# Six more modulation blocks reduced across the partitions by GpSimd instead of TensorE, with one accumulator for all of them

## What is computed

```python
mod = jax.nn.silu(c) @ w_ada[l] + b_ada[l]                 # 2048 x 12288
sh_a, sc_a, gt_a, sh_f, sc_f, gt_f = jnp.split(mod, 6, axis=-1)
h = rmsnorm(x, g_pre_attn[l]) * (1.0 + sc_a) + sh_a        # needed at once
...
x = x + gt_a * rmsnorm(mix @ w_out[l], g_post_attn[l])     # needed at the output projection
h = rmsnorm(x, g_pre_ffn[l]) * (1.0 + sc_f) + sh_f         # needed before the feed-forward part
f = (jax.nn.silu(h @ w_gate[l]) * (h @ w_up[l])) @ w_down[l]
x = x + gt_f * rmsnorm(f, g_post_ffn[l])
```

## Time and profile before

| | us |
|---|---|
| time, median of 3 runs (lowest, highest) | 2506.98 (2505.96, 2508.56) |
| time of the profiled execution | 2507.84 |
| its span | 2506.1 |
| PE busy | 2382.0 (95%) |
| DVE busy | 1670.5 (67%) |
| ACT busy | 1135.2 (45%) |
| POOL busy | 95.2 (4%) |

### The profile page before, as it was taken

How to read it: one execution, slowest core, us unless ns; L and a number is a source line. 1 busy time by engine, 2 the same in 40 slices (tenths; PEclk the granted TensorE clock), 3 DMA queues, 4 the chain that set the end, 5 groups by cost and what they waited for, 6 DMA issues and landing times.

```text
span 2506.1 us, 27346 instructions
## 1 busy us (share of the span) xinstructions
PE 2382.0 (95%) x10764; PEld 1966.3 (78%) x10764; DVE 1670.5 (67%) x1789; ACT 1135.2 (45%) x1473; POOL 95.2 (4%) x62
## 2 busy tenths in 40 slices
PE   2799999979999999899969999999999999999997
PEld 2577787868888888788858888888888888888886
DVE  6988898968888888755554555656555555555564
ACT  3345566554444444444453433443445544444453
POOL 1000000001111111300000000000000001000000
PEclk7899999989999999999989999999999999999999
DMA  8988788959999999755535655555566557665553
GB/s 297 366 298 310 269 289 335 350 181 334 325 335 327 327 329 325 267 188 198 191 125 167 208 180 181 183 189 176 199 205 205 198 193 256 205 196 190 186 190 111
DMA packets 255317, 600.52 MB, mean 240 GB/s; under 512 B 12313, under 2 KB 12633, under 8 KB 248673
## 3 DMA queue, kind: packets, MB, share of 16 engines
q1 hardware_dynamic: 252224, 589.43, 67.5%
q0 software_dynamic: 2976, 9.49, 1.2%
HBM read 596.74 MB, written 2.13 MB: 239 GB/s over the span
## 4 chain that ended last, share of the span: by engine, by line
PE 89%; DVE 6%; ACT 2%; DMA 2%; issue 1%; SPq 0%; DVEq 0%; ACTq 0%
PE PS L1181 19%; PE PS L1182 18%; PE PS L1187 18%; PE PS L1153 10%; PE PS L1156 10%; PE PS L1162 10%; DVE BIAS L1594 3%; DMA RAW<-in_w_in 1%; PE PS L1252 1%; DMA RAW<-in_w_ada 1%; DVE LO L1576 1%; ACT HI L687 1%; PE PS L1509 1%; PE PS L1278 0%; PE PS L1224 0%
## 5 line engine op out<-in xcount | busy, mean ns | idle before, releaser
L1576 DVE TENSOR_TENSOR LO<-RAW,HI 128x1024 fp32r<-128x1024 f32 x808 | 1013.8, 1260 | 726.2 <-ACT HI L687 724.9
L687 ACT ACTIVATE HI<-RAW 128x1024 fp32r<-128x1024 f32 x808 | 854.4, 1059 | 1213.3 <-PE PS L1187 746.8
L1181 PE MATMUL PS<-HI,XH 128*128 128x512 f32 x2176 | 871.1, 400 | 29.6 <-ACT HI L687 29.6
L1182 PE MATMUL PS<-HI,XL 128*128 128x512 f32 x2176 | 856.5, 394 | 0.0
L1187 PE MATMUL PS<-LO,XH 128*128 128x512 f32 x2176 | 585.9, 391 | 0.0
L1181 PEld LDWEIGHTS PS<-HI,XH 128*128 128x128 f32 x2176 | 413.3, 190 | 121.2 <-DVE XL L1720 20.9
L1187 PEld LDWEIGHTS PS<-LO,XH 128*128 128x128 f32 x2176 | 411.5, 189 | 87.6 <-DVE LO L1576 0.3
L1182 PEld LDWEIGHTS PS<-HI,XL 128*128 128x128 f32 x2176 | 414.0, 190 | 83.8 <-issue 1.0
L1594 DVE SCALAR_TENSOR_TENSOR BIAS<-RAW,CACT,BIAS 128x1024 f32<-128x1024 f32 x270 | 346.3, 1283 | 8.6 <-DMA RAW<-in_w_ada 1.4
L1153 PE MATMUL PS<-HI,XH 128*128 128x512 f32 x1056 | 328.5, 392 | 4.0 <-ACT HI L687 4.0
L1156 PE MATMUL PS<-HI,XL 128*128 128x512 f32 x1056 | 326.6, 391 | 0.0
(11 more groups left out here) (285 smaller groups left out, 998.6 us busy)
## 6 DMA issues: line engine op xcount, KB each, us to landing
RAW<-in_w_in SPq DMA_DIRECT2D x208, 1024.0 KB, 5.0
RAW<-in_w_ada SPq DMA_DIRECT2D x112, 1024.0 KB, 6.0
RAW<-in_w_gate SPq DMA_DIRECT2D x88, 512.0 KB, 4.5
RAW<-in_w_up SPq DMA_DIRECT2D x88, 512.0 KB, 5.5
RAW<-in_w_down SPq DMA_DIRECT2D x44, 1024.0 KB, 4.8
RAW<-in_w_ada SPq DMA_DIRECT2D x64, 512.0 KB, 6.0
RAW<-in_w_out SPq DMA_DIRECT2D x32, 1024.0 KB, 5.2
RAW<-in_w_proj_b SPq DMA_DIRECT2D x16, 1024.0 KB, 5.1
```

Source lines behind the costliest of these rows:

```text
L687: act.activation(HI[:, (it["half"] + hf) % HLS, :], RAW[:, it["slot"], hf * 1024:(hf + 1) * 1024], ACT.Copy).then_inc(s.hi_ready, 1)
L1181: pe.matmul(PS[:, bank + u, :], XH[:, 2 * n + kk, rows], hi, start=start and kk == 0, stop=False)
L1182: pe.matmul(PS[:, bank + u, :], XL[:, 2 * n + kk, rows], hi, start=False, stop=False)
L1576: dve.tensor_tensor(LO[:, slot, :], RAW[:, it["slot"], hf * 1024:(hf + 1) * 1024], HI[:, slot, :].bitcast(F32), ALU.subtract).then_inc(s.l ...
```

## The change

`ADA_BY_PE` goes from 10 to 4: TensorE sums groups 0 to 3 alone, GpSimd sums groups 4 to 17. So from group 4 on one accumulator `ACC` serves all groups, and the other is `SUM`. Groups 4, 5, 6 and 9 (sh_f and sc_f) go through memory: row 0 of `SUM` to `mod_dram`, back into `MODT` as 32 rows of 128, one transpose on TensorE into PSUM behind the last half of the first stage, and one add to `SHB`. Groups 7 and 8 (gt_a) are taken by VectorE from `SUM`, which has the sum in every partition, in 1024 columns beside h = 98 and 114. The scale of the second norm is computed behind the residual instead of ahead of it.

```diff
-ADA_BY_PE = 10
+ADA_BY_PE = 4
...
-SUMS_AT = {3: (1, None), 9: (2, None), 15: (3, None), 44: (4, None), 60: (5, None), 76: (6, None), 93: (7, 0), 95: (7, 1),
-           108: (8, 0), 110: (8, 1), 124: (9, None)}
-SUMS = [1, 2, 3, 4, 5, 6, 7, 9, 11, 12]
+SUMS_AT = {3: 1, 9: 2, 15: 3}
+SUMS = [1, 2, 3, 4]
...
                 wait(pool, s.sum_out, n * 16)
+                if a in (8, 9):
+                    pool.wait_ge(s.gga_ready, a - 7)
                 pool.partition_all_reduce(SUM, ACC, P, RADD).then_inc(s.acc_reduced, 1)
...
+            for a in (4, 5, 6):
+                reduce_ada(a)
             pool.wait_ge(s.qk_t, 16)
             pool.dma_start(G_ROW, g_post_attn.to_broadcast([P, D])).then_inc(s.rows_in, 16)
+            reduce_ada(7)
             pool.wait_ge(s.s_done, 24)
             pool.dma_start(B_ROW, b_ada[:, 4096:6144].to_broadcast([P, D])).then_inc(s.rows_in, 16)
-            for a in range(ADA_BY_PE, 16):
+            reduce_ada(8)
+            pool.wait_ge(s.cols_t, 2)
+            pool.dma_start(MODT[0:24, :], mod_dram[0, 0:3072].rearrange("(t p) -> t p", p=P)).then_inc(s.mod_in, 16)
+            reduce_ada(9)
+            pool.wait_ge(s.sum_out, 16 * 6)
+            pool.dma_start(MODT[24:32, :], mod_dram[0, 5120:6144].rearrange("(t p) -> t p", p=P)).then_inc(s.mod_in, 16)
+            for a in range(10, 16):
                 reduce_ada(a)
...
-            pe.wait_ge(s.ada_out, SUMS[-1])
+            pe.wait_ge(s.mod_in, 32)
+            bank_7_free()
+            pe.transpose(PS[:, 7, 0:32], MODT[0:32, :], IDENT[0:32, 0:32]).then_inc(s.mod_t, 1)
+            pe.wait_ge(s.ada_out, 5)
...
+            def ada_columns():
+
+                dve.wait_ge(s.mod_t, 1)
+                dve.tensor_tensor(SHB[:, 32:64], SHB[:, 32:64], PS[:, 7, 0:32], ALU.add).then_inc(s.ada_out, 1)
+                dve.wait_ge(s.ada_out, 5)
+
+            def ada_rows(a):
+
+                at = 1024 * (a - 7)
+                dve.wait_ge(s.acc_reduced, a - ADA_BY_PE + 1)
+                dve.wait_ge(s.rows_in, 32)
+                dve.tensor_tensor(GGA[:, at:at + 1024], SUM, B_ROW[:, at:at + 1024], ALU.add).then_inc(s.gga_ready, 1)
+                dve.wait_ge(s.gga_ready, a - 6)
+                link(dve.tensor_tensor(GGA[:, at:at + 1024], GGA[:, at:at + 1024], G_ROW[:, at:at + 1024], ALU.mult))
...
-            dve.wait_ge(s.ada_out, SUMS[-1])
-            dve.wait_ge(s.xh_ready, 8)
-            modulation(1, 48)
...
+            ada_columns()
+            modulation(1, 48)
```

More of the change, by code:

```diff
@@ L436, in build @@
             head_ms head_root mix_rstd mix_ready mix_t mtb_ready part_out wo_sq wo_out y0_ready rows_in
-            gg_in gg_ready post_done
+            gg_in gga_ready gg_ready post_done
             f_silu f_ready f_t xs_hi xs_lo m_in wif_hi wif_lo if_done if_ready if_t neg_f soft_f
@@ L651, in _ @@
             pool.dma_start(MASKB, k_mask_b).then_inc(s.mask_in, 16)
+            for a in (4, 5, 6):
+                reduce_ada(a)
             pool.wait_ge(s.qk_t, 16)
             pool.dma_start(G_ROW, g_post_attn.to_broadcast([P, D])).then_inc(s.rows_in, 16)
+            reduce_ada(7)
             pool.wait_ge(s.s_done, 24)
             pool.dma_start(B_ROW, b_ada[:, 4096:6144].to_broadcast([P, D])).then_inc(s.rows_in, 16)
[L657 removed]
+            reduce_ada(8)
[5 more added lines that the diff above has]
+            for a in range(10, 16):
                 reduce_ada(a)
+            pool.wait_ge(s.mod_t, 1)
             load_modulation(12, b_ada_2[0, 0:4096])
@@ L1244, in bank_7_free, with ada_sum @@
                 wait(pe, s.o_done, used[1])
-            def ada_sum(a, hf):
+            def ada_sum(a):
                 pe.wait_ge(s.ada_step, a * 16 + 16)
@@ L1249, in ada_sum @@
                 used[0] += 1
[L1250 to L1255, removed]
+                for t in range(8):
+                    m = pe.matmul(PS[:, 7, t:t + 1], acc_of(a)[:, t * P:(t + 1) * P], ONES[:, 0:1], start=True, stop=True,
+                                  skip_group_check=True)
                 m.then_inc(s.ada_sum, 1)
-            ada_sum(0, None)
+            ada_sum(0)
             sec = secs["first"]
@@ L1376, in beside_first @@
                 if h in SUMS_AT:
-                    ada_sum(*SUMS_AT[h])
+                    ada_sum(SUMS_AT[h])
             for h in range(sec.n_halves):
@@ L1433, in _ @@
                     if g == 10 and k + hf == 13:
-                        pe.wait_ge(s.mod_in, 32)
+                        pe.wait_ge(s.mod_in, 64)
                         pe.wait_ge(s.f_ready, 10)
@@ L1885, in beside_first @@
                 if h in (4, 10, 16):
[L1886 to L1892, removed]
+                    first_scale(SUMS_AT[h - 1])
+                if h in (98, 114):
+                    ada_rows(7 + (h == 114))
                 if h == 116:
@@ L1959, in _ @@
                         gated(g - 1)
-            dve.wait_ge(s.mod_t, 1)
+            dve.wait_ge(s.mod_t, 2)
             link(dve.tensor_copy(SHB[:], PS[:, 6, 0:64]))
```

## The result

The changed kernel takes 2517.7 us (median of 6 runs, 2517.41 to 2519.93) against 2507.25 us (6 runs, 2505.96 to 2508.56): ratio 1.0044, interval 1.0031 to 1.0056, so slower by 0.44%. Its profiled execution has a span of 2515.6 us against 2506.1.

A forecast was written before the change was run, and what follows sets the result against it. TensorE was taken to bound the kernel (89% of the chain). Group terms 0.4 + 2.3 + 1.8 - 0.4 + 1.1 - 1.8 = +3.4 us, plus 1.1 for the clock: +4.5, median 2511.5 us, range 2504.5 to 2519.

The forecast's parts named there:

- the forecast's own case: The main forecast for the whole kernel: median 2511.5 us, spanning 2508 to 2516 us; chance 0.55.
- the third rival: VectorE's row maximum also blocked (+4.3 us), or release only at reduction's end (+5.1): 2516 to 2517 us, both 2521; chance 0.22.
- What is removed: On TensorE, four column sums (about 1.9 us each) and four row sums (0.91 each) go: 11.2 us.
- Who is held, and for how long: VectorE instructions with two SBUF operands stand still during a reduction, let go 5.3 us behind its start.
- Group 6: Beside h = 76 only an unblocked row maximum; +0.3 us, replaced by +1.8 for the later chain over VectorE and DMA.
- the prediction's own signs of being wrong: Unblocked L1802, TensorE wait at h = 74, lower clock in several stretches, or `LO` making TensorE wait behind h = 110.
- The wait for the accumulator: A group's first step waits for the reduction's end, 7.3 us behind the last step; group 5's moves 4.2 us.
- Group 9: Column sum beside h = 124 gone, `LO` still about 1 us ahead: -1.8 us; way through memory costs 0.
- The clock: TensorE clock dips behind new waits: none from below, two (3.4 us) from above; taken as 1.1 us.
- the lead absorbs it: VectorE's lateness doesn't reach TensorE at groups 4 and 5: -0.9 us, 2506.1 us without a clock dip; chance 0.18.
- TensorE's time comes back: Reductions cost nothing TensorE waits for, so its removed sums count in full on the chain: 2497.6 us; chance 0.05.
- More is blocked than I take: Heading of the third rival: more VectorE work blocked by reductions, or for longer; 2516 to 2517 us; chance 0.22.

The follow-up runs named there:

- the last run: Changed kernel with in-place reductions in four pieces, two accumulators, gate rows in four operations of 512 columns, group 8's reduction after the last factors: 2503.01 us, ratio 0.9985.

## Why the prediction was right, and where it was not

The direction, slower, and the range (2504.5 to 2519) held; the forecast of +4.5 us was less than half of the +10.5 measured. That the range held is in part luck: the forecast's own case ended at 2516, and what lies above it stood there for the third rival, whose two mechanisms did not occur. By its steps:

- *What is removed.* Right: 1.8 us for a column sum and 0.9 for a row sum in the table against 1.9 and 0.91. For group 7 I had forecast only -0.4, since the chain ran over VectorE there, and that held: -1.8 at h = 94 and 96, then +1.4 at h = 100, where TensorE waits for VectorE and ScalarE anyway. The 1.4 is not the price of two operations of 1024 columns in one place, as I took it to be before the last run: with the rows split it was 1.8.
- *Who is held, and for how long.* The release "5.3 us behind the reduction's start" held at all four places (5.1 to 5.3), and so did the later starts behind groups 5 and 8: 4.2 and 2.9 us forecast, 4.1 and 2.7 measured. Behind group 4 it was 3.0 in place of 2.3: the group ended 0.8 us nearer to TensorE's work than in the kernel before (2.4 us later, with TensorE 1.6 later).
- *Group 6.* Wrong. "Beside h = 76 there is only a row maximum": there is also the clamp, which I passed over because it has one operand in SBUF. The row maximum is indeed not held; the clamp ahead of it is. The wait of TensorE at h = 74, one of the prediction's own signs of being wrong, came, though not for the reason given there. Without the held clamp the trace showed just what I had forecast for this place, +0.4 us with the sum gone (forecast 0.3), and 1.1 later on. I had put 1.8 there for the chain over the DMA, so the sum was off by only 0.7 (4.3 - 1.8 against 1.8), by luck.
- *The wait for the accumulator.* It was to move the first step of group 5 by 4.2 us. The first step starts 7.8 us behind the group's end, but does not wait for the reduction there: the held instruction ahead of it in VectorE's order had made it as late already. It becomes the bound when the stops are short.
- *Group 9.* "`LO` still has about 1 us of lead" was a little too much: +0.9 us at h = 124.
- *The clock.* This is the step that failed most in size. "I take 1.1" stood on one dip moved and another perhaps. In the profiled execution every one of the four waits brought a dip of its own, 7.5 us, and only 3.1 of before went away: +4.4 in place of +1.1, over three of the missing six. The kernel with filled waits shows it: 5.8 to 6.5 us less. Between two ends, none and two dips, I had left out the case that each wait has one, though I had priced one at 1.7 us from the earlier trace rows, and had named a lower clock in more than one stretch as a sign of being wrong. In other executions some of the same waits had no dip, so 7.5 is the value of this execution, not a fixed one.

The rest of the six is not of one cause. The waits cost 2.2 us more than forecast (0.8 behind group 4, 0.7 behind group 6, 0.9 behind group 9, 0.2 less behind group 8). The medians differ by 0.9 us more than the two profiled executions, which are 9.6 apart. And in these stand +1.6 ahead of the change's first place and -2.2 in the stages behind it. Of the rivals, "the lead absorbs it" and "TensorE's time comes back" are refuted (the latter's 2497.6 is what short reductions gave, 2498.9). "More is blocked than I take" was right in its heading and wrong in both its forms: not the row maximum, and not until the reduction's end. Its 2516 to 2517 lay nearest to the 2517.7 all the same.

On that last point the Trainium skill (SBUF — State Buffer, "Who interferes with whom") also names VectorE's `tensor_scalar` among the forms that can take the port pair which GpSimd shares. The trace agrees: the clamp took 4.56 us from SBUF and 0.28 from PSUM. On the length it doesn't: held for the whole instruction would be until 6.9 to 7.0 us behind the reduction's start, and it was 5.1 to 5.3. The reduction's recorded end is borne out by the first step that waited for it behind group 8, which started 0.1 us later (470.05).

## What to carry to other kernels

Work moved to an engine that idles (GpSimd) is not free when it holds up a neighbour (VectorE) for which a third engine (TensorE) waits: ask which instructions of the neighbour can't run beside it, not only two-operand ones, and how late each may be. Make what excludes others short instead of placing it well, and let nothing wait for its end: eight pieces in two accumulators took GpSimd nearly twice as long and brought the whole time 20 us down, while moving the one long piece only moved the loss. And price a wait of TensorE of 1 to 5 us in a stretch at full clock with what may follow it: here 1.5 to 2.7 us of lower clock each, behind 11 of 14 such waits.

## What the runs showed of the hardware that I had not expected

- A whole reduction of 128x1024 takes 6.9 to 7.0 us beside VectorE's two-operand work (6.11 in the change for group 9, 7.15 at most in the other kernels) and holds VectorE up to 5.1 to 5.3 us behind its start; pieces of 256 columns take 1.8 to 2.5 us, of 128 columns about 1.6 beside VectorE's work, and of 32 columns 1.3 to 1.4, or 0.53. Between pieces VectorE gets its turn.
- A TENSOR_SCALAR with one SBUF input is held (4.56 us, 5.03 us); one from PSUM, a RECIPROCAL of 128x8 (0.20) and the row maximum from PSUM and SBUF are not.
- Waits of TensorE of 1.2 to 5.1 us in a stretch at full clock were followed by the lower level in 11 of 14 cases, and in none of 7 where useless matmuls filled them.
- The kernel before varies by more than the six runs beside the change showed: the 67 runs beside the experiments lay between 2501.95 and 2513.75 us. In the traces, the first 17 halves, which no version touches, end at 144.9 to 150.9 us.
